# Transformer block kernel, one core: sums of squares gathered while the residual is updated, roots and reciprocals on token columns, first weight turn slice by slice

## What is computed

```python
def rmsnorm(x, w):
    xf = x.astype(jnp.float32)
    y = xf * lax.rsqrt(jnp.mean(xf * xf, axis=-1, keepdims=True) + EPS)
    return (y * w.astype(jnp.float32)).astype(x.dtype)

# per layer, with shift, scale and gate from the conditioning vector:
#   x = x + gate * mixer(rmsnorm(x) * (1 + scale) + shift)
#   x = x + gate * swiglu(rmsnorm(x) * (1 + scale) + shift)
# and rmsnorm once more on the latent tokens at the end
def swiglu(h, w1, w2):
    gu = h @ w1
    return (jax.nn.silu(gu[..., :D_FF]) * gu[..., D_FF:]) @ w2
```

## Time and profile before

| | us |
|---|---|
| median of 3 runs | 3844.21 |
| lowest, highest | 3841.21, 3849.33 |
| the profiled execution, its own time | 3844.28 |
| span in its profile | 3842.4 |
| busy in the span: PE, PEld, DVE, ACT, POOL | 3414.2, 2828.8, 1618.0, 1056.1, 660.3 |
| granted TensorE clock, mean | 0.932 |

### The profile page before, as it was taken

The page is one execution under the profiler, slowest core; times in us unless marked ns, Lnnn a source line. Parts: engine busy times, 40 slices in busy tenths (PEclk is TensorE's granted clock), DMA queues, the critical chain, the costliest instruction groups (busy, mean ns, idle before and its releaser), DMA issues. The chain is left out here.

```text
span 3842.4 us, 56889 instructions
## 1 busy us (share of the span) xinstructions
PE 3414.2 (89%) x21948; PEld 2828.8 (74%) x21948; DVE 1618.0 (42%) x2653; ACT 1056.1 (27%) x1931; POOL 660.3 (17%) x764
## 2 busy tenths in 40 slices
PE   6989857878889999999998989757887889999998
PEld 3878646766758888888886878646775678888885
DVE  4465676632242322223236465675533233322234
ACT  3343135512132121121213243135512231122112
POOL 1133753222000000000001142753221000000000
PEclk8989868988899999999999999968997999999999
DMA  4456283096301111111111456283295011111111
GB/s 170 143 187 201 71 274 103 15 282 204 136 17 38 38 38 38 38 38 38 38 39 76 143 187 201 79 274 89 70 259 181 33 38 49 49 49 49 46 47 61
DMA packets 245757, 396.43 MB, mean 103 GB/s; under 512 B 76099, under 2 KB 148035, under 8 KB 245190
## 3 DMA queue, kind: packets, MB, share of 16 engines
q1 hardware_dynamic: 239750, 374.05, 30.9%
q0 software_dynamic: 5824, 19.93, 1.4%
HBM read 280.30 MB, written 101.52 MB: 99 GB/s over the span
## 5 line engine op out<-in xcount | busy, mean ns | idle before, releaser
L905 PE MATMUL ffn_bank<-ffn_h_hi,ffn_w_hi 128*128 128x512 f32 (+1 forms) x1760 | 650.6, 370 | 18.1 <-DVE ffn_h_lo L323 18.1
L908 PE MATMUL ffn_bank<-ffn_h_lo,ffn_w_hi 128*128 128x512 f32 (+1 forms) x1760 | 650.0, 369 | 0.0
L909 PE MATMUL ffn_bank<-ffn_h_hi,ffn_w_lo 128*128 128x512 f32 (+1 forms) x1760 | 649.5, 369 | 0.0
L815 PE MATMUL frt_acc<-frt_w_hi,frt_h_hi 128*128 128x472 f32 x960 | 375.5, 391 | 47.7 <-DVE frt_w_lo L695 26.0
L905 PEld LDWEIGHTS ffn_bank<-ffn_h_hi,ffn_w_hi 128*128 128x128 f32 x1760 | 333.3, 189 | 75.8 <-DVE ffn_h_lo L323 18.1
L909 PEld LDWEIGHTS ffn_bank<-ffn_h_hi,ffn_w_lo 128*128 128x128 f32 x1760 | 333.0, 189 | 55.6
L908 PEld LDWEIGHTS ffn_bank<-ffn_h_lo,ffn_w_hi 128*128 128x128 f32 x1760 | 333.2, 189 | 55.2
L899 DVE TENSOR_TENSOR ffn_w_lo<-ffn_raw,ffn_w_hi 128x1024 fp32r<-128x1024 f32 x132 | 161.7, 1225 | 503.1 <-ACT ffn_w_hi L895 497.9
L815 PE MATMUL frt_acc<-frt_w_hi,frt_h_lo 128*128 128x472 f32 x960 | 368.6, 384 | 0.0
L815 PE MATMUL frt_acc<-frt_w_lo,frt_h_hi 128*128 128x472 f32 x960 | 366.0, 381 | 0.0
L905 PE MATMUL ffn_bank<-ffn_a_hi,ffn_w_hi 128*128 128x512 f32 (+1 forms) x880 | 324.4, 369 | 0.8 <-DVE ffn_a_lo L973 0.8
(11 more groups left out here) (332 smaller groups left out, 5492.5 us busy)
## 6 DMA issues: line engine op xcount, KB each, us to landing
ffn_raw<-w_ffn SPq DMA_DIRECT2D x132, 512.0 KB, 3.5
x<-ada_w SPq DMA_DIRECT2D x15, 2048.0 KB, 9.3
proj<-frt_out SPq DMA_DIRECT2D x120, 236.0 KB, 2.0
x<-proj SPq DMA_DIRECT2D x60, 384.0 KB, 4.5
frt_raw<-w_in SPq DMA_DIRECT2D x96, 236.0 KB, 4.4
pack<-frt_side SPq DMA_DIRECT2D x80, 256.0 KB, 2.5
met_pr<-proj SPq DMA_DIRECT2D x20, 704.0 KB, 6.3
met_vn<-pack SPq DMA_DIRECT2D x20, 640.0 KB, 6.4
```

Of the source, the lines that this page charges most:

```text
L815: mm = pe.matmul(acc[q % NA][:, 0:GW], a[:, k, tok], b[:, k, :], start=(k == 0 and i == 0), stop=(k == KC - 1 and i == 2))
L905: mm = pe.matmul(out, w_hi, b_hi, start=first, stop=False)
L908: pe.matmul(out, w_hi, b_lo, start=False, stop=False)
L909: return pe.matmul(out, w_lo, b_hi, start=False, stop=last)
```

## The change

Everywhere but in the first layer's `front`:

- `mixed` and the last turn of `ffn` get a `Squares` object. After DVE has added to x, ACT squares that piece and DVE adds the square to a buffer `total` of 128 by 1280. In `mixed` DVE does so right behind its addition, in `ffn` one piece later. ACT's rounding of weights in `mixed` now stands behind the squares of a chunk.
- The norm that follows (`normed_from`, and `final`) starts from `total`: one matmul for each tile of 128 tokens, with `total` as the stationary operand and 2 columns of 1/1024, puts the means on token partitions; one root over 128 by 2 columns a tile, one reciprocal; then DVE writes identity times root times 1024 for each slice over `total` (`laid`), and one matmul with the 1/1024 matrix spreads it over all partitions, into PSUM (`spread`). L315 and L2351 then read their factor there. A root on one element ahead of it (`warm`) brings the table load forward.
- Weight units 0 and 1 of `ffn` are split ahead of slice 0 and behind slice 0 of the norm; PE's first turn goes slice by slice, both units in each, and waits chunk by chunk (`pe_first`). The loops of PE are split so that this turn stands by itself.
- `front`, in both layers: the projection waits for `h_ready` chunk by chunk.

```diff
+def normed_from(nc, st, x, total, scale, mod, shift0, lo, hi_t, lo_t, ones, eps, ident, scaled, spread, sums):
...
+    def pe_norm(pe):
+        for g in range(lo // P, TILES):
+            mm = pe.matmul(sums[:, 2 * g:2 * g + 2], total[:, g * P:(g + 1) * P], ones[:, 0:2], start=True, stop=True)
+        mm.then_inc(summed, 1)
+        for s, (t0, n) in enumerate(slices):
+            pe.wait_ge(laid, s + 1)
+            pe.matmul(spread[s][:, 0:n], ones[:], total[:, t0:t0 + n], start=True, stop=True).then_inc(spread_s, 1)
+
+    def act_norm(act, first=None, second=None):
+        act.activation(warm[:], eps[:], ACT.Sqrt)
+        act.wait_ge(summed, 1)
+        act.activation(root[:, whole, :], sums[:, 2 * whole.start:2 * TILES].rearrange("p (g a) -> p g a", a=2), ACT.Sqrt, bias=eps[:]).then_inc(rooted, 1)
+        if first:
+            first(act)
+        for s, (t0, n) in enumerate(slices):
...
+                act.wait_ge(scaled_s, i + 1)
+                act.activation(hi_t[:, k, t0:t0 + n], scaled[i % 2][:, 0:n], ACT.Identity, bias=mod[:, shift0 + k, v:v + 1]).then_inc(rounded, 1)
+            if s == 0 and second:
+                second(act)
+
+    def dve_norm(dve, first=None, second=None):
+        dve.wait_ge(rooted, 1)
+        dve.reciprocal(root[:, whole, :], root[:, whole, :]).then_inc(inverted, 1)
+        dve.wait_ge(inverted, 1)
+        for s, (t0, n) in enumerate(slices):
+            g, each = tiles(s), [P, n // P, P]
+            dve.scalar_tensor_tensor(total[:, t0:t0 + n].rearrange("p (g n) -> p g n", n=P), ident.unsqueeze(1).broadcast_to(each), float(DM),
+                                     root[:, g, 0:1].broadcast_to(each), ALU.mult, ALU.mult).then_inc(laid, 1)
+        if first:
+            first(dve)
...
+class Squares:
...
+    def square(self, act, m, s):
...
+        if j >= 2:
+            act.wait_ge(self.gathered, j - 1)
+        to = self.total[:, t0:t0 + n] if m == 0 else self.scratch[j % 2][:, 0:n]
+        act.activation(to, self.x[:, m, t0:t0 + n], ACT.Square).then_inc(self.squared, 1)
+
+    def gather(self, dve, m, s):
...
+        if m:
+            dve.wait_ge(self.squared, i + 1)
+            dve.tensor_tensor(self.total[:, t0:t0 + n], self.total[:, t0:t0 + n], self.scratch[j % 2][:, 0:n], ALU.add).then_inc(self.gathered, 1)
...
@@ front, project
-                    if g == 0:
-                        pe.wait_ge(h_ready, (1 + sum(t * P >= t0 + n for t0, n in slices)) * KC)
+                    at = sum(t * P >= t0 + n for t0, n in slices)
...
+                        if g == 0:
+                            pe.wait_ge(h_ready, at * KC + k + 1)
...
@@ ffn
+        def pe_first(pe):
+            for s, (t0, ln) in enumerate(slices):
+                for u in range(2):
+                    if s == 0:
+                        pe.wait_ge(w.ready[u], 1)
+                    for k in range(KC):
+                        if u == 0:
+                            pe.wait_ge(h_ready, s * KC + k + 1)
...
-        def dve_down(dve, n, b, m0, each, more):
+        def dve_down(dve, n, b, m0, each, last):
+            behind = None
...
+                        if last:
+                            if behind:
+                                squares.gather(dve, *behind)
+                            behind = (m, s)
...
-                w.rest(dve, 0, 0)
-                dve_norm(dve)
-                w.rest(dve, 1, 0)
+                dve_norm(dve, first=lambda dve: w.rest(dve, 0, 0), second=lambda dve: w.rest(dve, 1, 0))
...
@@ mixed, scalar
-                with act.Fori(0, TURNS) as n:
-                    for u in range(2):
-                        w.round(act, u, n)
+                for u in range(2):
+                    w.round(act, u, 0)
+                for m in range(KC):
+                    for s in range(NS):
+                        act.wait_ge(free[m % 2][s], m // 2 + 1)
+                        squares.square(act, m, s)
+                    if m + 2 < KC:
+                        w.round(act, m % 2, m // 2 + 1)
```

More of the change, by code:

```diff
@@ L342, in front @@
+def front(nc, layer, x, x_landed, x_copy, w_in, proj, mod, amix, ones, eps, conv_w, small, mats, tri, pack, feat, diag, inv, tot, total):
     with Stage(nc, f"frt{layer}") as st:
@@ L909, in three_passes, with ffn @@
     return pe.matmul(out, w_lo, b_hi, start=False, stop=last)
-def ffn(nc, layer, x, lo, units, mod, affn, ones, eps):
+def ffn(nc, layer, x, lo, units, mod, affn, ones, eps, ident, total):
     J = 4
@@ L2250, in mixed @@
         weights_first = st.sem("weights_first")
+        squares = Squares(st, x, total, [st.sb(f"sq{i}", [P, 512])[:] for i in range(2)], slices)
         with nc.Block() as block:
@@ L2300, in _, with final @@
                         w.rest(dve, m % 2, m // 2 + 1)
-def final(nc, x, norm_w, out, ones, eps):
+def final(nc, x, norm_w, out, ones, eps, ident, total):
+    slices = token_slices(CTX)
     with Stage(nc, "fin") as st:
         nw = st.sb("nw", [P, KC])
-        sq = [st.sb(f"sq{i}", [P, 512]) for i in range(2)]
-        root, inv = st.sb("root", [P, 512]), [st.sb(f"inv{i}", [P, 512]) for i in range(2)]
         y = st.sb("y", [P, KC, LAT])
-        ms = [st.ps(f"ms{s}", [P, 512]) for s in range(2)]
-        s = signals(st, "set_in squared summed rooted inverted done stored")
+        root, warm = st.sb("root", [P, TILES, 2]), st.sb("warm", [P, 1])
+        sums = st.ps("sums", [P, 2 * TILES])
+        spread = [st.ps(f"spread{s}", [P, 512]) for s in range(2)]
+        s = signals(st, "set_in summed rooted inverted laid spread done stored")
+        whole = slice(CTX // P, TILES)
+        tiles = lambda i: slice(slices[i][0] // P, (slices[i][0] + slices[i][1]) // P)
         with nc.Block() as block:
@@ L2342, in _ @@
+                mm.then_inc(s["summed"], 1)
+                for i, (t0, n) in enumerate(slices):
+                    pe.wait_ge(s["laid"], i + 1)
+                    pe.matmul(spread[i][:], ones[:], total[:, t0:t0 + n], start=True, stop=True).then_inc(s["spread"], 1)
             @block.vector
             def _(dve):
-                dve.wait_ge(s["set_in"], 16)
[L2345 to L2349, removed]
+                dve.wait_ge(s["rooted"], 1)
@@ new lines, in _ @@
+                dve.reciprocal(root[:, whole, :], root[:, whole, :]).then_inc(s["inverted"], 1)
+                dve.wait_ge(s["inverted"], 1)
+                for i, (t0, n) in enumerate(slices):
+                    g, each = tiles(i), [P, n // P, P]
+                    dve.scalar_tensor_tensor(total[:, t0:t0 + n].rearrange("p (g n) -> p g n", n=P), ident.unsqueeze(1).broadcast_to(each), float(DM),
+                                             root[:, g, 0:1].broadcast_to(each), ALU.mult, ALU.mult).then_inc(s["laid"], 1)
```

158 lines of the change are left out of this document (118 added, 40 removed).

## The result

The changed kernel takes **3803.24 us** (median of 6 runs, 3793.41 to 3816.46) where the kernel before takes 3840.31 (6 runs, 3833.12 to 3849.33): a ratio of 0.9902, 95% interval 0.9887 to 0.9918. It is faster by 37 us; the forecast was 76.8 us, 3768, and the range ended at 3784. Half of the gain is missing.

A forecast was written before the change was run, and what follows sets the result against it. PE bounds the kernel (busy 3414 of 3842 us), so gains lie only in its waits at stage starts. From 3844.28 us: -0.7 - 28.7 - 17.9 - 23.6 - 11.7 + 5.8 = -76.8, so 3767.5, stated as 3768; range 3758 to 3784.

The forecast's parts named there:

- The step that failed: Dense feed-forward rows: a bank of 24 matmuls costs 5.44 us, and no norm can help inside that stretch.
- PE's total work hardly changes: Whole kernel: the squares' matmuls are removed where PE had idle time.
- The two first turns: First turn of each `ffn`, norm overlapped slice by slice: -28.7 us in the first, -23.6 us in the second.
- The second `front`: Norm beside POOL's weight splits, scaling reading PSUM: tile 3 earlier by 17.9 us, or 13.3 if the pace stays.
- head: Start of each new norm: sums 3.3 us for ten tiles, 2.7 for eight; root and reciprocal 0.65; then `laid` and spreading.
- The final norm: Last stage: first output piece 5.6 us after the start, -11.7 us in all.
- The tails: Ends of `mixed` and `ffn`, four times: a square, an addition and handshakes add 1.45 us at each barrier, +5.8 us.
- The clock: Rival: half-fed first turns of `ffn` keep PE at 1.2 GHz, making dense banks cost 10.2 us; 3776 to 3793, 10%.
- The backlog: Rival: additions and gatherings fall behind in the last turns of `ffn`, 4.4 us; 3772, 8%.
- Contention stays: Rival: the second `front`'s norm keeps its pace beside POOL; 3772, or 3776 if POOL slows as well; 12%.
- not overlapped: Rival: PE's slice-wise turn wins nothing and the `ffn` stages keep their waits in another place; 3785, 3%.

The follow-up runs named there:

- a_back2: The kernel of `a_back` (changed kernel with 896 unused bytes ahead of the feed-forward weight units) run once more as a base: 3769.12 us, ratio 0.9814.
- b_moved: The kernel before, with only the feed-forward weight tiles moved to the addresses they have in the changed kernel: 3874.09 us, ratio 1.0072.
- a_nosq: `a_back` without squares and gatherings for seven of eight feature chunks in `mixed` and the last turn of `ffn`: 3761.62 us, ratio 0.9793.
- a_oldloop: The changed kernel with PE's loops of `ffn` as before, without the peeled slice-wise first turn: 3830.80 us, ratio 0.9971.
- a_back: The changed kernel with 896 unused bytes per partition ahead of the feed-forward weight units: 3774.53 us, ratio 0.9813.
- m_scan: PE alone, no model: 23 rows of 96 matmuls with shifted weights and moving operand, repeated with DVE and ACT writing; 226.7 to 234.3 ns a matmul.

## Why the prediction was wrong, by its own steps

Every span is taken from the stage's first instruction, in us:

| step | before | after | a_back2 | forecast | after less before |
|---|---|---|---|---|---|
| first `ffn`, to the turn's last product | 74.9 | 45.8 | 45.6 | -28.7 | -29.1 |
| first `ffn`, from there to the next stage | 884.3 | 900.0 | 885.8 | +1.45 | **+15.7** |
| second `front`, to tile 3 | 56.7 | 40.9 | 41.2 | -17.9 | -15.8 |
| second `ffn`, to the turn's last product | 62.7 | 37.6 | 37.1 | -23.6 | -25.0 |
| second `ffn`, from there to the next stage | 698.9 | 720.7 | 700.4 | +1.45 | **+21.8** |
| final norm, to the span's end | 31.3 | 21.0 | 20.2 | -11.7 | -10.3 |

**The step that failed** is the first one: "A bank of 24 matmuls of 512 columns thus costs 5.44 us, and no norm can help inside that stretch", and with it "PE's total work hardly changes". The sum put the two dense rows of `ffn` at nothing, since it took the price of a bank from the kernel before as fixed. No norm can help there, but a moved buffer can hurt: a bank costs 5.59 us at the new addresses. The change's lines on `sil`, `sq`, `root` and `warm` were in the diff and got no price, not even a bound. It was worth 34.7 us of the 38.1 that are missing, and neither the range nor a rival held it; with the weights at the old remainder the kernel is at 3769 and 3775 us in two sets.

**The two first turns** were right: 29.1 for 28.7, and 25.0 for 23.6. In the second, 25 is what the prediction's own terms give if unit 1 runs at full clock (3081.4 and one bank of 5.44); it had taken the half clock, and the clock was 1.00. DVE's chunk is 1.45 us and PE follows it at that step; from 3044.51 on PE has no gap, so the second turn's weights come in time as well.

**The second `front`** gave 15.8 us to tile 3, not 17.9. The scaling's reading of PSUM did what L781 promised, and only the rests stretch beside POOL (`after`, timeline):

```profile
2061.40 0.48 DVE L394 SCALAR_TENSOR_TENSOR frt_side<-x,amix,frt_b_s 128x256 f32<-128x256 f32 x1
2061.80 0.90 DVE L406 SCALAR_TENSOR_TENSOR frt_h_lo<-frt_side,mod,frt_h_hi 128x256 fp32r<-128x256 f32 x1
```

That is what the Trainium skill, "SBUF — State Buffer", section "Who interferes with whom", says: a vector instruction with at most one SBUF input and no two-port mode doesn't contend with GpSimd. The trace agrees, with 0.48 where it was 1.29. The mechanism was right, the head mis-sized. The sums of the ten tiles are done 4.0 us after the start (root at 2055.74) where 2.7 were taken, 1.3 of the 2.1 us. Of that, 0.6 is a slip: 2.7 is the prediction's figure for eight tiles, and for ten it has 3.3. The rest is the clock, as in the final norm below. The other 0.8 is a balance: `laid` took 0.2 more than the sum has, slice 0 9.9 us for 8.7, slices 1 and 2 23.4 for 24.0.

From tile 3 to the last projection matmul it is 357.8 us before and 362.2 after. Whether the change has a part in these 4 us is not shown: a_back2 has 357.5, but the other nine runs with the changed `front` 360.0 to 362.3, and `b_moved`, with the old one, 358.6. In the first `front` all thirteen runs lie between 359.4 and 362.7.

**The final norm** has its first piece 7.05 us after the start, not 5.6. The sums took 3.5 us for 2.7, and from the first spreading matmul to the first piece it is 2.2 us (3787.59 to 3789.79) for 1.5. The sums were priced at 0.24 us a tile, two instructions, and that holds only while the clock is full. These are the sixteen instructions of the eight tiles in the final norm, `after` first, then `a_nosq` (windows; busy times of PE, PEld, DVE, ACT, POOL, PEclk, DMA, GB/s):

```profile
3782.74:3786.30 3.56, 3.48 (x16) 3.39 (x16) 0.00 (x0) 1.49 (x3) 0.00 (x0) 0.51 0.02 1
```
```profile
3740.33:3742.30 1.97, 1.91 (x16) 1.83 (x16) 0.00 (x0) 1.46 (x3) 0.00 (x0) 1.00 0.04 2
```

At a granted clock of 1.00 they start 0.112 us apart, at 0.50 0.213. In all four stages of `after` the clock falls to 0.50 within 0.9 us of the first sum, so the head's length depends on the moment of that fall; the prediction named the case and took a middle value. In `a_nosq`, with the sums at 1.00, the first piece comes 5.5 us after the start.

**The tails** are 1.4 us each, as priced. From the last addition to the next stage's first instruction, in the order of time, it is 1.96, 1.64, 1.94 and 1.60 us before, and 3.38, 3.06, 3.36 and 3.04 now. `a_nosq`, which keeps the squares of one chunk, takes back 1.16 of each, and shows that nothing piles up ahead.

**The rivals.** *The clock*: the half-fed turn kept 1.00 (`after`, windows; busy times of PE, PEld, DVE, ACT, POOL, PEclk, DMA, GB/s):

```profile
3037.00:3042.00 5.00, 3.07 (x11) 1.60 (x11) 4.78 (x8) 2.83 (x5) 0.00 (x0) 1.00 0.00 0
...
2054.00:2071.00 17.00, 13.07 (x35) 7.34 (x35) 14.38 (x23) 5.69 (x11) 16.04 (x16) 0.70 1.02 403
```

PE ran 3 matmuls in every 1.45 us in the second `ffn` and stayed at 2.4 GHz; in the first it was granted 1.00 from 1117.0 us to the turn's end. In `front`, where it waited for the norm's chunks and POOL's splits and then 7.98 us for tile 3, it was granted 0.70 up to 2071 us and 0.83 from there to 2092, in the mean; it still reached that wait, so the norm and not the clock sets tile 3. *The backlog*: in a_back2 the last turn's additions start 1.36 us apart, PE's own step (3732.55, 3733.91, 3735.27, 3736.63); none. *Contention stays* and *not overlapped* fell with the rows above, and a_oldloop shows what the latter would have cost.

## What to carry to other kernels

When a change frees, adds or reorders buffers, list the addresses of both operands of every dense matmul before and after, and compare their difference modulo 256 bytes; keep it at 0 with a pad (128 bytes did as well as 896), and check the count of matmuls in a window of an untouched stretch, since waits and busy shares don't show the loss. Price a change of allocation like a change of code, above all where it touches stages that hold 45% of the span, as the two `ffn` do here. The slice-wise turn and the norm on token columns are worth 68 and 72 us in two sets (`a_back`, `a_back2`) with 896 unused bytes. All this is measured for matmuls of 512 moving columns in fp32r; in `front`, with 472, the distance was worth 0.9 ns a matmul.

## What the runs showed of the hardware

- A 128x128 by 128x512 fp32r matmul at full clock takes 226.7 ns, 228.9, 232.4 or 233.3 to 234.3 ns depending on the distance in SBUF between its weights and its moving operand, modulo 256 bytes (`m_scan`). Idle or busy DVE and ACT change it by 0.1 ns at most. At a granted clock of 0.50 it is 426.7 ns at distance 0 and at 128 alike (`before`, `b_moved`). Which of the two reads gives way, and whether bf16 shows it, was not tried.
- The Trainium skill, "SBUF — State Buffer", section "SBUF: two separate sides", says that PE never waits on anyone at its SBUF ports. For DVE and ACT beside it the scan agrees, within 0.1 ns. PE by itself is another matter: its pace depends on the distance between its own two operands, and `b_moved` is 0.72% slower by addresses alone.
- With moving rows of 472 columns and tokens as weights, stepping through the remainders by 96 bytes costs 0.9 ns a matmul (214.2 for 213.3), not 4.
- A matmul of two columns on fresh fp32 weights is two instructions, which start 0.112 us apart at a granted clock of 1.00 and 0.213 at 0.50. Ten token tiles took 2.6 to 4.4 us at a stage's start, by the moment at which the clock fell.
- In `after` the clock falls while a stage's sums run: PE is idle for 3.1 to 3.4 us at the barrier and starts at 1.00, and the fall to 0.50 comes 0.8, 0.5, 0.7 and 0.1 us after the first sum of the four stages.
